# Prompt attention of a hybrid decoder layer: group 0 by consecutive tokens, groups 1 and 2 by residue, softmax shares exchanged through DRAM

## The reference, cut to what matters

```
A_WINDOWS = (128, 512, 2048); A_DILATIONS = (1, 4, 16); A_HEADS = 8; A_HEAD_DIM = 128
# group g, head h: token t reads the keys t - j*d, j = 0..window//d
scores = einsum('qe,ke->qk', q, k) * 128 ** -0.5     # masked by distance
p, lse = softmax over the keys, and its log-sum-exp
wts = softmax(stack(lses of the 3 groups), axis=0)
o_a = sum over groups of wts * outs                  # then times silu(z_a)
```

## Time and profile before

| | before |
|---|---|
| median of 3 runs | 3024.98 us |
| the profiled execution: its own time | 3022.8 us |
| its span in the trace | 3021.0 us |
| PE busy | 2968.5 us (98%) |
| DVE, ACT, POOL busy | 1875.7, 867.3, 1214.9 us |
| prompt attention on PE | from 538 to about 1516 us |

### The profile page before, as it was taken

The page is one execution under the profiler, slowest core; times in us unless marked ns, Lnnn a source line. Parts: engine busy times, 40 slices in busy tenths (PEclk is TensorE's granted clock), DMA queues, the critical chain, the costliest instruction groups (busy, mean ns, idle before and its releaser), DMA issues.

```text
span 3021.0 us, 51650 instructions
## 1 busy us (share of the span) xinstructions
PE 2968.5 (98%) x22252; PEld 2821.6 (93%) x22252; DVE 1875.7 (62%) x2020; ACT 867.3 (29%) x1239; POOL 1214.9 (40%) x576
## 2 busy tenths in 40 slices
PE   6999999999999999999999999999999999999998
PEld 4898899999999999999999999999999989999886
DVE  3303788988785788878887756766668665211302
ACT  3121122233233233233222242333323343211312
POOL 1133344433333434344445544444444344444332
PEclk9999999999999999999999999999999999999999
DMA  8879786554446786646567666756657666876643
GB/s 326 334 275 353 300 295 243 201 204 137 140 142 218 264 290 232 204 175 256 230 248 254 244 228 213 236 195 236 212 194 240 232 201 216 293 258 247 252 174 139
DMA packets 220457, 704.81 MB, mean 233 GB/s; under 512 B 26739, under 2 KB 129899, under 8 KB 170795
## 3 DMA queue, kind: packets, MB, share of 16 engines
q1 hardware_dynamic: 157686, 471.33, 44.7%
q0 software_dynamic: 5248, 174.60, 14.3%
q10 hardware_dynamic: 57296, 55.59, 5.5%
HBM read 630.85 MB, written 245.17 MB: 290 GB/s over the span
## 4 chain that ended last, share of the span: by engine, by line
PE 93%; DMA 3%; DVE 2%; issue 1%; ACT 0%; SPq 0%; POOL 0%; DVEq 0%; ACTq 0%; POOLq 0%
PE acc L1380 24%; PE acc L1382 24%; PE acc L1381 24%; DMA side<-in_keys_t 2%; PE ps_s L1249 1%; PE ps_s L1534 1%; PE ps_s L1419 1%; PE ps_w L1439 1%; DVE side L1792 1%; PE ps_s L1500 1%; PE ps_t L1394 1%; PE ps_s L1427 1%; PE ps_s L1618 1%; PE ps_s L1619 1%; PE ps_s L1620 1%; DMA w_raw<-in_w_ada_t 1%
## 5 line engine op out<-in xcount | busy, mean ns | idle before, releaser
L895 POOL TENSOR_TENSOR w_lo<-w_raw,w_hi 128x1024 fp32r<-128x1024 f32 (+1 forms) x416 | 1076.3, 2606 | 1758.5 <-ACT w_hi L946 1758.5
L1380 PE MATMUL acc<-act,w_hi 128*128 128x288 f32 x5744 | 1716.4, 299 | 2.6 <-POOL w_lo L895 2.5
L1382 PE MATMUL acc<-act,w_lo 128*128 128x288 f32 x5744 | 1691.4, 294 | 0.0
L1381 PE MATMUL acc<-act,w_hi 128*128 128x288 f32 x5744 | 1691.2, 294 | 0.0
L1380 PEld LDWEIGHTS acc<-act,w_hi 128*128 128x128 f32 x5744 | 1077.7, 188 | 37.0 <-issue 28.5
L1381 PEld LDWEIGHTS acc<-act,w_hi 128*128 128x128 f32 x5744 | 1078.0, 188 | 1.1
L1382 PEld LDWEIGHTS acc<-act,w_lo 128*128 128x128 f32 x5744 | 1077.2, 188 | 0.0
L946 ACT ACTIVATE w_hi<-w_raw 128x1024 fp32r<-128x1024 f32 (+1 forms) x418 | 403.8, 1015 | 483.3 <-PE acc L1382 191.2
L1821 DVE TENSOR_TENSOR side<-side 128x2048 f32<-128x2048 f32 x96 | 283.5, 2953 | 95.9 <-DMA side<-in_vals_t 83.2
L1014 ACT ACTIVATE ev<-acc 128x576 f32<-128x576 f32 x144 | 93.8, 651 | 802.8 <-PE acc L1382 798.9
L1792 DVE TENSOR_TENSOR side<-side 128x2048 f32<-128x2048 f32 x96 | 279.1, 2907 | 72.3 <-DMA side<-in_keys_t 69.2
(11 more groups left out here) (333 smaller groups left out, 2771.7 us busy)
## 6 DMA issues: line engine op xcount, KB each, us to landing
w_raw<-in_w_in_t SPq DMA_DIRECT2D x160, 1024.0 KB, 7.6
out_s_kv<-in_cache_a_w POOLq DMA_DIRECT2D x80, 1632.0 KB, 9.0
side<-in_keys_t SPq DMA_DIRECT2D x52, 1024.0 KB, 7.6
side<-in_vals_t SPq DMA_DIRECT2D x52, 1024.0 KB, 8.2
out_s_kv<-in_cache_a_w POOLq DMA_DIRECT2D x24, 1344.0 KB, 8.3
w_raw<-in_w_ada_t SPq DMA_DIRECT2D x24, 1024.0 KB, 7.5
w_raw<-in_w_gate_t SPq DMA_DIRECT2D x16, 1024.0 KB, 10.2
w_raw<-in_w_o_b_t SPq DMA_DIRECT2D x16, 1024.0 KB, 7.9
```

The source lines that it names most:

```text
L895: nc.gpsimd.tensor_tensor(dst, raw[:, SLOT[s], ks, 0:cols], wh[:, u % 2, ks, 0:cols].bitcast(F32), ALU.subtract).then_inc(lo, 1)
L1380: nc.tensor.matmul(out, wh[:, c, k, 0:cols], high, start=(k == 0), stop=False)
L1381: nc.tensor.matmul(out, wh[:, c, k, 0:cols], low, start=False, stop=False)
L1382: mm = nc.tensor.matmul(out, wl[:, c, k, 0:cols], high, start=False, stop=(k == kt - 1))
```

## The change

Group 0 is now computed by blocks of 128 consecutive tokens: step r of a head takes queries 128r to 128r+127 and reads only the block itself and the one before it. Groups 1 and 2 are still computed by residue class, but ACT writes q and k of these groups to memory in class order already when it copies a unit out of PSUM (three copies instead of one, with a step of 4 in PSUM), so that scores read them with step 1. A step's rows are now two different sets of tokens, and so each set has its own maximum and sum. The joint softmax needs them in the other's order: per head, SP writes the maxima and sums to DRAM and reads them back permuted, DVE works out the weights, scales the unnormalised outputs of the whole head at once, PE transposes them (four blocks, twice), and DVE gates and adds. Masks shrink, eleven semaphores become eleven others with fewer waits per step, the load of the gate (za) moves from offset 4 to offset 8 of its head.

```
+
+        def head_of(half, offset):
+
+            j = half - ATT0 - 3 * PACE - offset
+            return j // (4 * PACE) if 0 <= j < 4 * H * PACE and j % (4 * PACE) == 0 else None
...
-                    if j == 4 * PACE * h + 4:
+                    if half == ATT0 + 4 * PACE * h + 3 * PACE + 1:
+                        sp.wait_ge(at_e, 5 * h + 4)
+                        own = stats(h)[:, 0]
+                        sp.dma_start(S["stats"][h, 0].rearrange("z (s p) -> p z s", p=P), own[:, 0], allow_slow_non_contiguous=True).then_inc(ls_out, 16)
+                        sp.dma_start(S["stats"][h, 1].rearrange("z (p s) -> p z s", p=P), own[:, 1]).then_inc(ls_out, 16)
+                    if half == ATT0 + 4 * PACE * h + 3 * PACE + 2:
+                        other = stats(h)[:, 1]
+                        sp.wait_ge(ls_out, 32 * (h + 1))
+                        sp.dma_start(other[:, 0], S["stats"][h, 1].rearrange("z (s p) -> p z s", p=P), allow_slow_non_contiguous=True).then_inc(ls_in, 16)
+                        sp.dma_start(other[:, 1], S["stats"][h, 0].rearrange("z (p s) -> p z s", p=P)).then_inc(ls_in, 16)
...
+                if BY_CLASS[u]:
+                    rows = ev[:, c, 0:SEQ].rearrange("p (r i) -> p r i", r=4)
+                    for part, (i0, i1) in enumerate(((0, HALF // 4), (HALF // 4, P))):
+                        nc.scalar.activation(rows[:, :, i0:i1], acc[c][:, part, 0:4 * (i1 - i0)].rearrange("p (i r) -> p r i", r=4), ACT.Copy)
+                    nc.scalar.activation(ev[:, c, SEQ:TOK], acc[c][:, 1, SEQ - HALF:HALF], ACT.Copy).then_inc(evac, 1)
...
+                    for a in range(2):
+                        cols = slice(P if a == 0 and r == 0 else 256 * a, 256 * (a + 1))
+                        mm = nc.scalar.activation(prow[:, cols], prow[:, cols], ACT.Exp, bias=neg_max[:, a:a + 1], scale=SCALE,
+                                                  accum_out=stats(h)[:, 0, a, 1, r:r + 1])
+                    mm.then_inc(at_e, 1)
...
+                if at := step_of(half, 4):
+                    h, r = at
+                    act_e.wait_ge(at_o, 4 * h + r + 1)
+                    after(act_e, at_g, 3 * h)
+                    nc.scalar.activation(oU[:, r, :, :], ps_w[:, 0:2 * P].rearrange("p (a e) -> p a e", a=2), ACT.Copy).then_inc(at_c, 1)
...
+                if (h := head_of(half, 6)) is not None:
+                    pe.wait_ge(ls_v, 7 * h + 7)
+                    after(pe, at_g, 3 * h - 1)
+                    for x in range(4):
+                        mm = nc.tensor.transpose(turned[:, x * P:(x + 1) * P], oU[:, x, 0, :], ident[:, :])
+                    mm.then_inc(at_t, 1)
+                if (h := head_of(half, 8)) is not None:
+                    pe.wait_ge(at_g, 3 * h + 1)
+                    for x in range(4):
+                        mm = nc.tensor.transpose(turned[:, x * P:(x + 1) * P], oU[:, x, 1, :], ident[:, :])
+                    mm.then_inc(at_t, 1)
...
+                    cls, first = slice(r * P, (r + 1) * P), max(0, r - 1) * P
...
-                    nc.tensor.matmul(ps_s[:, 0:512], qk[:, 0, r:SEQ:4], qk[:, 3, :], start=True, stop=True)
-                    nc.tensor.matmul(ps_s[:, 512:640], qk[:, 1, r:SEQ:4], qk[:, 4, r:SEQ:4], start=True, stop=True)
-                    nc.tensor.matmul(ps_s[:, 640:768], qk[:, 2, r:SEQ:4], qk[:, 5, r:SEQ:4], start=True,
+                    after(pe, at_c, 2 * n - 1)
+                    nc.tensor.matmul(ps_s[:, 2 * P - (r + 1) * P + first:2 * P], qk[:, 0, cls], qk[:, 3, first:(r + 1) * P], start=True, stop=True)
+                    nc.tensor.matmul(ps_s[:, 2 * P:3 * P], qk[:, 1, cls], qk[:, 4, cls], start=True, stop=True)
+                    nc.tensor.matmul(ps_s[:, 3 * P:4 * P], qk[:, 2, cls], qk[:, 5, cls], start=True,
...
+                    for y in range(0 if r else 1, 4):
                         mm = nc.tensor.transpose(ps_s[:, y * P:(y + 1) * P], prow[:, y * P:(y + 1) * P], ident[:, :])
...
-                    nc.tensor.matmul(ps_w[:, P:2 * P], pT[:, 4, :], vP[:, 4 + r, :], start=True, stop=False)
-                    for x in range(4):
-                        nc.tensor.matmul(ps_w[:, P:2 * P], pT[:, x, :], vP[:, x, :], start=False, stop=False)
-                    nc.tensor.matmul(ps_w[:, P:2 * P], pT[:, 5, :], vP[:, 8 + r, :], start=False, stop=True).then_inc(at_o, 1)
+                    else:
+                        nc.tensor.matmul(ps_w[:, 0:P], pT[:, 0, :], vP[:, r - 1, :], start=True, stop=False)
+                    nc.tensor.matmul(ps_w[:, 0:P], pT[:, 1, :], vP[:, r, :], start=(r == 0), stop=True)
+                    nc.tensor.matmul(ps_w[:, P:2 * P], pT[:, 2, :], vP[:, 4 + r, :], start=True, stop=False)
+                    nc.tensor.matmul(ps_w[:, P:2 * P], pT[:, 3, :], vP[:, 8 + r, :], start=False, stop=True).then_inc(at_o, 1)
...
+                if (h := head_of(half, 3)) is not None:
+                    both = stats(h)
+                    dve.wait_ge(ls_in, 32 * (h + 1))
+                    dve.wait_ge(at_e, 5 * h + 4)
+                    TT(top, both[:, 0, :, 0, :], both[:, 1, :, 0, :], ALU.max).then_inc(ls_v, 1)
+                    dve.wait_ge(ls_v, 7 * h + 1)
+                    TT(share, both[:, :, :, 0, :], top.unsqueeze(1).broadcast_to((P, 2, 2, 4)), ALU.subtract).then_inc(ls_v, 1)
...
+                    TT(parts, share, stats(h)[:, :, :, 1, :], ALU.mult).then_inc(ls_v, 1)
...
+                    TT(weight, share[:, 0], total, ALU.mult).then_inc(ls_v, 1)
+                    dve.wait_ge(ls_v, 7 * h + 6)
+                    dve.wait_ge(at_c, 8 * h + 8)
+                    TT(oU, oU, weight.rearrange("p a s -> p s a").unsqueeze(3).broadcast_to((P, 4, 2, E)), ALU.mult).then_inc(ls_v, 1)
...
+                    TT(oU[:, :, 0, :], turned.rearrange("p (s e) -> p s e", s=4), za.rearrange("p (s e) -> p s e", s=4), ALU.mult).then_inc(at_g, 1)
...
+                    by_class = za.rearrange("p (i r) -> p r i", r=4)
+                    TT(by_class, turned.rearrange("p (r i) -> p r i", r=4), by_class, ALU.mult).then_inc(at_g, 1)
+                    dve.wait_ge(at_g, 3 * h + 2)
+                    TT(za.rearrange("p (s e) -> p s e", s=4), za.rearrange("p (s e) -> p s e", s=4), oU[:, :, 0, :], ALU.add).then_inc(at_g, 1)
...
-                    TT(prow[:, 0:SEQ], ps_s[:, 0:SEQ], mprompt[:, 3 - r:3 - r + SEQ], ALU.add).then_inc(at_m, 1)
-                    TT(prow[:, SEQ:768], ps_s[:, SEQ:768], mprompt[:, MASK0:MASK0 + 2 * P], ALU.add).then_inc(at_m, 1)
-                    dve.wait_ge(at_m, 3 * n + 2)
-                    nc.vector.reduce_max(stat[:, 0:1], prow, AX).then_inc(at_m, 1)
...
-                if at := step_of(half, 1):
...
-                    nc.vector.reciprocal(stat[:, 3:4], stat[:, 2:3]).then_inc(at_i, 1)
...
-                    TS(oN, ps_w[:, P:2 * P], stat[:, 3:4], None, ALU.mult).then_inc(at_on, 1)
...
-                    TT(za[:, r:SEQ:4], ps_w[:, 2 * P:3 * P], za[:, r:SEQ:4], ALU.mult).then_inc(at_g, 1)
...
+                    TT(prow[:, lo:2 * P], ps_s[:, lo:2 * P], mprompt[:, lo:2 * P], ALU.add).then_inc(at_m, 1)
...
+                    nc.vector.reduce_max(own[:, 0, 0, r:r + 1], prow[:, lo:2 * P], AX).then_inc(at_m, 1)
+                    nc.vector.reduce_max(own[:, 1, 0, r:r + 1], prow[:, 2 * P:4 * P], AX).then_inc(at_m, 1)
+                    dve.wait_ge(at_m, 5 * n + 4)
+                    TS(neg_max, own[:, :, 0, r], -SCALE, None, ALU.mult).then_inc(at_m, 1)
```

More of the change, by code:

```diff
@@ L52, in shape_constants @@
     i = np.arange(P)
-    prompt = np.zeros((P, MASK0 + 2 * P), np.float32)
-    lag = 4 * i[:, None] + 3 - np.arange(MASK0)[None, :]
-    prompt[:, :MASK0] = np.where((lag >= 0) & (lag <= 128), 0, neg)
     dist = i[:, None] - i[None, :]
-    prompt[:, MASK0:MASK0 + P] = np.where(dist >= 0, 0, neg)
-    prompt[:, MASK0 + P:] = np.where((dist >= 0) & (dist % 4 == 0), 0, neg)
+    prompt = np.zeros((P, 3 * P), np.float32)
+    prompt[:, 0:P] = np.where(dist <= 0, 0, neg)
+    prompt[:, P:2 * P] = np.where(dist >= 0, 0, neg)
+    prompt[:, 2 * P:] = np.where((dist >= 0) & (dist % 4 == 0), 0, neg)
     b, t = np.arange(SAMP) // NT, np.arange(SAMP) % NT
@@ L188 @@
 STORED = [kind in "qkzrA" for kind in KINDS]
+BY_CLASS = [kind in "qk" and g > 0 for kind, g, _ in UNITS]
 STORES = [[sum(1 for v in range(u + 1) if v % 2 == c and STORED[v]) for u in range(NU)] for c in range(2)]
@@ L416, in phase_all, with stats @@
         X, Y, Z = (ps_t, ps_w), ps_s[:, 0:512], ps_s[:, 512:1024]
+        def stats(h):
+            return lse[:, 32 * (h % 2):32 * (h % 2) + 32].rearrange("p (w a z s) -> p w a z s", w=2, a=2, z=2)
+        top = lse[:, 64:72].rearrange("p (a s) -> p a s", a=2)
+        share = lse[:, 72:88].rearrange("p (w a s) -> p w a s", w=2, a=2)
+        parts = lse[:, 88:104].rearrange("p (w a s) -> p w a s", w=2, a=2)
+        total = lse[:, 104:112].rearrange("p (a s) -> p a s", a=2)
+        weight = lse[:, 112:120].rearrange("p (a s) -> p a s", a=2)
```

(14 more changed lines are left out.)

99 lines of the change are left out of this document (49 added, 50 removed).

## The result

The changed kernel takes 3030.24 us (median of 20 runs, 3019.68 to 3036.09), the kernel before beside it 3023.1 (20 runs, 3015.9 to 3026.62): a ratio of 1.0027, 95% interval 1.002 to 1.0035. That is slower by 7 us by the medians and 8 by the ratio. The forecast was 2983 with a range of 2970 to 3002, so it was wrong, in sign too. The profiled execution has a span of 3026.4 us against 3021.0 before, that is +5.4.

A forecast was written before the change was run, and what follows sets the result against it. The prediction took PE, busy 98% of the span, as the bound. 3022.8 us less 50 from PE's list plus 8 of new waits gave 2981 profiled, 2983 for the median, which is 2 higher; range 2970 to 3002.

The forecast's parts named there:

- PE's list: Work PE issues for attention: fewer and cheaper matmuls and transposes over eight heads, 50 us shorter, bounds 35 to 52.
- Each price: PE's score matmuls, start to start: 0.22 us for 128 columns and 0.45 for 256.
- the bounds were 15 apart: PE's saving: 35 us if step 1 does not make groups 1 and 2's scores cheaper, otherwise 50; dear scores had 0.11.
- ACT's copy in three parts: ACT's copy of q or k units of groups 1 and 2: 0.9 to 1.3 us instead of 0.65, hidden from PE.
- The wait at the head's weights: PE waiting for DVE's weights in the next head's first step: together 8 us, bounds 0 and 25.
- That is a round trip of 24 us; from there each us costs PE one us per head.: Threshold worked out at head 0: shares' trips through DRAM shorter than this do not touch PE.
- I take 17: Shares' store to DRAM and load back: 17 us, from a range of 12.4 to 20, up to 28.
- The number of pieces, not their size, made most of rows 8 and 9: Trace rows of 1024 runs of 256 B, stored in 9.7 us and loaded in 10.3, used to price single elements.
- The rival that covered it: Shares' round trip from about 29 us on makes the kernel slower than before; chance 0.06.
- SP is blocked for the store's 10 us only and is free before 651.94: At head 0, SP's wait for the shares' store ends before its next weight load is issued.
- DVE needs about 0.7 + 1.2 us: DVE's operations for a head's weights, leaving them ready 0.8 us after the old place's time.
- I put DVE's sum at nothing: DVE's removed and added work per head, both near 11 us, was taken to cancel.

The follow-up runs named there:

- Experiment 2: Changed kernel with the exchange moved in whole rows (runs of 16 B), the token permutation left out: 2986.74 us, 0.9886 of before.
- pairs: Changed kernel with a token's maximum and sum side by side, so permuted transfers move 512 pieces of 8 B, not 1024 of 4 B: 2991.2 us.
- experiment 10: Kernel with pairs, with DVE's six operations for a head's weights issued ahead of that half's grain of key or value products: 2976.15 us, 0.9846 of before.
- Experiments 2 and 5: Changed kernel with exchange in runs of 16 B (2986.74 us), and changed kernel with 512 pieces of 8 B in the permuted transfers (2991.2 us).
- ACT's queue: Changed kernel with the same exchange issued by ACT instead of SP: 3029.82 us, 1.0026 of before.

## Why the prediction was wrong

**PE's list: right.** "PE's list gets 50 us shorter" was measured as 46.5 less busy time, with slower clock in it; without the exchange the busy time is 52.1 less. Each price held: 0.22, 0.43 for 0.45, and the saving by step 1 alone 16 us where the bounds were 15 apart. ACT's copy in three parts stayed hidden: PE's waits for ACT at L1448 are 7.3 us in the changed kernel, but 0.7 without the exchange and 0.4 with whole rows, and both have that copy.

**The wait at the head's weights: wrong, 46.6 us instead of 8.** The sum of the profiled executions closes: -46.5 busy, +51.9 standing still, +5.4. Forecast was -42. Of the miss of 47, the waits at L1456 are 38.6, the other waits 5.3, and 3.5 is missing from the gain in busy time, which without the exchange is 52.1: the lower clock behind each wait.

The step that failed is what the shares' trip does to PE, which the forecast put at nothing: "That is a round trip of 24 us; from there each us costs PE one us per head." By that rule the trips of 16.2 to 19.2 us at heads 0 to 5 cost nothing and those of 25.2 and 25.1 at heads 6 and 7 one us each. PE waited 8.26 and 8.39 at heads 3 and 4, with trips of 19.2 and 18.3, and 18.50 and 11.48 at heads 6 and 7. The parts of it:

- "I take 17" for the trip came true by luck. "The number of pieces, not their size, made most of rows 8 and 9" priced the store at 9.7 us and the load at up to 10.3; the store took 12.8 to 18.2 until the load could be issued, and the loads landed in 2.1 to 7.7. Two errors of opposite sign gave the sum. Experiment 2's 43 us hang on the store. The rival that covered it asked for "some 15 us by itself", which I called above every row and gave 0.06; but it expected trips of 29 us and more, and the kernel became slower with less.
- The rule counts only DVE's own wait for the shares. "SP is blocked for the store's 10 us only and is free before 651.94" holds at head 0, where SP is at the next weights at 642.19; at head 6 it comes to them at 1370.85. And the chunk issued right behind the store lands in 13.6 to 16.7 us instead of 6.8 to 9.6. DVE runs dry on both, and neither is in the sum.
- I worked the slack out at one head and took it for all. Even at head 0 it was smaller than 24 us says: with a trip of 17.1 us the weights were ready 1.1 us before PE came.
- "DVE needs about 0.7 + 1.2 us" and "I put DVE's sum at nothing" took the lengths of operations that nothing disturbs. At heads 3, 4, 6 and 7 they take 3.9 to 4.8 us more, where POOL works. The grain of 4.6 us ahead of them was in the forecast's times, but not as something that could be moved: without the exchange the waits are 12.6 us, and with pairs, the exchange and the grain moved behind the weights (experiment 10), 3.9.

The Trainium skill (DMA: Bandwidth & Descriptors, Rules for kernel authors) warns of a last dimension that is not contiguous. I cited it as speaking against the store and then gave it no weight. Experiments 2 and 5 agree with it, for the store far more than for the load, where 1024 single elements landed in 3.0 us (median).

**What is shown, and what is not.** Taking the elements out of the exchange gives 43 us, taking it out altogether 47, and moving DVE's weights ahead 29 us with single elements and 17 with pairs. They overlap, since both shorten the same lateness. So that small pieces in the exchange cause the loss is shown by taking them out; how the loss divides among the late shares, SP's late issues, the late chunk and DVE's stretched operations is read from the traces, not tried, and so is that the stretching is POOL's doing. Why ACT's queue made the loads slower stays open too.

## What to carry to other kernels

Price a DMA by a row with pieces of the same number and the same size; without such a row, the high end belongs in the forecast. When a wait is put into a queue, list for every occurrence what stands behind it on that queue and when its consumer runs dry: the head with the most slack tells nothing of the one with the least. And before a consumer is moved later, look whether the producer has a long piece of work ahead of it that nobody is waiting for. Moving that was worth 29 us with single elements and 17 with pairs, where the later place was worth 20 and 6; larger pieces alone gave 38.

## What the runs showed of the hardware

**Half clock behind a short stop.** In the waits of 8 us and more the granted clock falls, and PE's products take twice as long for 2.7 to 4.7 us after them (windows of PE: length, busy, clock, DMA share and GB/s), as here behind the waits that end at 1019.62 and 1395.47:

```profile
1020.00:1022.00 2.00, 2.00 (x11) 0.50 0.90 381
1022.00:1024.00 2.00, 2.00 (x12) 0.65 0.67 197
1395.00:1397.00 2.00, 1.53 (x8) 0.50 0.84 209
1397.00:1399.00 2.00, 2.00 (x11) 0.53 1.41 610
1399.00:1401.00 2.00, 2.00 (x17) 1.00 0.48 197
```

That is 1.2 in place of 2.4 GHz, and half speed for 2.7 to 4.7 us loses some 1.4 to 2.4 us on top of each such wait, after 8.26 us as after 18.50. The engine had run at 1.00 up to the wait at 1376.97. So a wait of 8 us costs 10 to 11. A shorter one can cost as much on top: in experiment 10's kernel the wait of 3.88 us that ends at 1357.02 is followed by

```profile
1359.00:1361.00 2.00, 2.00 (x11) 0.50 0.71 254
```

and the clock is back at 1.00 only at about 1362.8.

**Small DVE operations beside POOL.** Over the traces of the changed kernel and its ten variants, the head's two-input operations of 8 and 16 columns took 0.15 to 0.18 us in all 293 cases with POOL idle. Of the 131 that began while POOL was at work, 83 took more than 0.5 us and the longest 5.05; the median is 2.06. The reciprocal of 8 columns, with one input, took 0.20 in all 24 such cases. But not every one-input operation passes: the scaling of two maxima (L2005, 128x2) took 0.17 in all 194 cases with POOL idle and 0.53 to 2.31 in all 157 that began with POOL at work, as here beside POOL's L921 of 650.67 to 655.43:

```profile
653.44 2.02 DVE L2005 TENSOR_SCALAR small<-lse 128x2 f32<-128x2 f32 x1
```

The Trainium skill (Trainium Architecture — The Big Picture, What this means for kernel authors) says that DVE and GpSimd contend for one shared pair of ports, by an exclusive lock and not a split of bandwidth. The traces agree, since 8 columns lose 2 us and not a share of 0.17. 48 of the 131 lost nothing, and why they and the reciprocal don't is not shown here.
